# Where three steps ahead of a gated delta rule stand in the order of a fused two-block kernel

## What is computed

```python
q = jnp.repeat(l2_norm(q), rep, axis=2) * DN_HEAD_DIM ** -0.5
k = jnp.repeat(l2_norm(k), rep, axis=2)
...
decay = jnp.exp(jnp.where(incl, gc[..., :, None] - gc[..., None, :], -jnp.inf))
kk = jnp.einsum("bhncd,bhnjd->bhncj", k, k)
m = jnp.where(strict, beta[..., :, None] * kk * decay, 0.0) + jnp.eye(C, dtype=f32)
...
sol = lax.linalg.triangular_solve(m, rhs, left_side=True, lower=True, unit_diagonal=True)
```

```python
q = rms_norm(xq.reshape(B, S, XA_HEADS, XA_DIM), qn_g)
s = jnp.einsum("bthd,bmhd->bhtm", q, k).astype(jnp.float32) * XA_DIM ** -0.5
```

## Time and profile before

| | us |
|---|---|
| median of 3 runs | 3015.46 (3014.51 to 3021.64) |
| the profiled execution | 3011.83 |
| its span | 3010.0 |
| TensorE busy | 2836.4 (94%) |
| VectorE busy | 1903.9 (63%) |
| ScalarE busy | 1411.2 (47%) |
| GpSimd busy | 386.0 (13%) |
| mean granted clock of TensorE, as a share of 2.4 GHz | 0.973 |

### The profile page before, as it was taken

The page is one execution under the profiler, slowest core; times in us unless marked ns, Lnnn a source line. Parts: engine busy times, 40 slices in busy tenths (PEclk is TensorE's granted clock), DMA queues, the critical chain, the costliest instruction groups (busy, mean ns, idle before and its releaser), DMA issues.

```text
span 3010.0 us, 46274 instructions
## 1 busy us (share of the span) xinstructions
PE 2836.4 (94%) x19298; PEld 2672.0 (89%) x19298; DVE 1903.9 (63%) x2814; ACT 1411.2 (47%) x2387; POOL 386.0 (13%) x360
## 2 busy tenths in 40 slices
PE   6999989889889999999989999998999999999997
PEld 6999989888888998999979999997888899987785
DVE  5546648533323544655456865776888888878786
ACT  5346543555654433444344204343555555555454
POOL 0000010211111000003100002221122211112320
PEclk9999989999999999999999999999999999999998
DMA  4443444422223554444434458998999988899894
GB/s 185 169 154 140 169 131 167 154 77 94 85 94 112 198 186 166 167 169 162 154 114 169 156 204 322 374 357 312 366 361 371 366 319 322 321 350 349 319 350 147
DMA packets 109680, 668.46 MB, mean 222 GB/s; under 512 B 25777, under 2 KB 26313, under 8 KB 31553
## 3 DMA queue, kind: packets, MB, share of 16 engines
q1 hardware_dynamic: 83808, 496.08, 45.2%
q0 software_dynamic: 24512, 164.97, 15.0%
q10 hardware_dynamic: 1152, 4.47, 0.4%
HBM read 651.54 MB, written 13.30 MB: 221 GB/s over the span
## 4 chain that ended last, share of the span: by engine, by line
PE 72%; DVE 12%; DMA 8%; ACT 7%; issue 2%; POOL 0%; SPq 0%; DVEq 0%; ACTq 0%
PE PS L1027 71%; DMA raw<-in_pv 4%; DVE WL L1641 4%; DVE m L1632 3%; DMA m<-in_pv,keep 3%; ACT m L2322 2%; ACT WH L2337 2%; ACT L2322 1%; DVE m L1841 1%; DVE m L2162 1%; DMA raw<-in_w_kv 1%; DVE m L1838 0%; PE PS L1030 0%; ACT m L2323 0%; DVE m L1660 0%
## 5 line engine op out<-in xcount | busy, mean ns | idle before, releaser
L1641 DVE TENSOR_TENSOR WL<-raw,WH 128x1024 fp32r<-128x1024 f32 x804 | 985.5, 1234 | 650.6 <-ACT WH L2337 649.6
L2337 ACT CAST WH<-raw 128x1024 fp32r<-128x1024 f32 x804 | 837.5, 1046 | 551.5 <-PE PS L1027 390.2
L1027 PE MATMUL PS<-m_4096r,WH 128*128 128x256 f32 x5184 | 997.3, 293 | 29.9 <-DVE m L1632 14.7
L1027 PEld LDWEIGHTS PS<-m_4096r,WH 128*128 128x128 f32 x5184 | 827.8, 196 | 53.2 <-DVE m L1632 16.1
L1027 PE MATMUL PS<-m_4096r,WL 128*128 128x256 f32 x2592 | 743.6, 287 | 0.0
L1027 PE MATMUL PS<-m_8192r,WH 128*128 128x256 f32 (+1 forms) x2560 | 559.7, 312 | 17.5 <-issue 11.1
L1027 PE MATMUL PS<-WH,m_896r 128*128 128x512 f32 x1536 | 523.1, 393 | 28.2 <-DVE m_896r L2255 27.9
L1027 PEld LDWEIGHTS PS<-m_4096r,WL 128*128 128x128 f32 x2592 | 507.6, 196 | 0.0
L1027 PEld LDWEIGHTS PS<-m_8192r,WH 128*128 128x128 f32 x2560 | 397.6, 193 | 20.3 <-issue 11.7
L1027 PE MATMUL PS<-m_8192r,WL 128*128 128x192 f32 (+1 forms) x1792 | 404.3, 272 | 0.0
L1027 PE MATMUL PS<-WL,m_896r 128*128 128x512 f32 x1024 | 400.8, 391 | 0.0
(11 more groups left out here) (234 smaller groups left out, 1857.7 us busy)
## 6 DMA issues: line engine op xcount, KB each, us to landing
raw<-in_pu SPq DMA_DIRECT2D x128, 1024.0 KB, 6.8
raw<-in_pv SPq DMA_DIRECT2D x128, 1024.0 KB, 8.0
raw<-in_w_qkv SPq DMA_DIRECT2D x48, 1024.0 KB, 4.8
raw<-in_w_o SPq DMA_DIRECT2D x48, 1024.0 KB, 4.8
raw<-in_w SPq DMA_DIRECT2D x40, 1024.0 KB, 4.8
raw<-in_w_z SPq DMA_DIRECT2D x32, 1024.0 KB, 4.8
raw<-in_w_kv SPq DMA_DIRECT2D x16, 1024.0 KB, 4.8
raw<-in_w_q SPq DMA_DIRECT2D x16, 1024.0 KB, 4.8
```

Source lines behind the costliest of these rows:

```text
L1027: return e.matmul(o, l, x, start=start, stop=stop)
L1641: tt(WL[:, k, :], raw[:, n % NRAW, h * 1024:h * 1024 + 1024], WH[:, k, :].bitcast(F), ALU.subtract).then_inc(S["lo"], 1)
L2337: e.copy(WH[:, k, :], raw[:, n % NRAW, h * 1024:h * 1024 + 1024]).then_inc(S["hi"], 1)
```

## The change

- The cross attention's scores, and all steps of `cross` after them, come one yield later.
- The squares are summed two at a time with one eighth after each pair, instead of six with three eighths. From `rn_root` to `iv_turn` two eighths pass instead of none, and three follow instead of six. In all 17 eighths pass in `qk_norm` instead of 18.
- ScalarE's part of `iv_decay` is a step of its own, `iv_exp`, that comes later in the order than VectorE's differences. The eighths of `invert` stay 35 up to `iv_scale`.

Since `qk_norm` takes one eighth less, every later step up to the last group's end stands one eighth earlier against the units. No instruction is added or removed, on any engine.

```diff
     def cross(self):
         yield from self.head_norm("q")
+        yield
         for h in range(4):
...
     def qk_norm(self, st):
         for i in range(24):
             self.do("rn_sum", i)
-            if i % 6 == 5:
+            if i % 2 == 1:
                 yield
         self.do("rn_root")
+        yield
+        yield
         self.do("iv_turn")
+        yield
         yield
         yield
         st["n"] = True
...
         for b in range(3):
             self.do("iv_decay", b)
-            yield 3
-        yield 20
+            yield 2
+            if b:
+                self.do("iv_exp", b - 1)
+            yield 2
+        self.do("iv_exp", 2)
+        yield 17
...
         for _ in self.qk_norm(st):
-            for _ in range(3):
-                next(fz)
+            next(fz)
...
-            def iv_decay(b):
+            def iv_exp(b):
                 x = iv_e[:, b, :, :]
                 a.wait_ge(*at("iv_gap", b + 1))
                 a.step(act(x, x, ACT.Relu))
                 a.own()
                 act(x, x, ACT.Exp, scale=-1.0).then_inc(S["iv_exp"], 1)
```

More of the change, by code:

```diff
@@ L2714, in scalar_program @@
                   "v_out": v_out, "z_out": z_out, "rn_root": rn_root, "iv_turn": iv_turn,
-                  "iv_decay": iv_decay, "dn_decay": dn_decay, "dn_uc": dn_uc, "dn_w": dn_w, "dn_u": dn_u_, "dn_y": dn_y, "dn_yss": dn_yss,
+                  "iv_exp": iv_exp, "dn_decay": dn_decay, "dn_uc": dn_uc, "dn_w": dn_w, "dn_u": dn_u_, "dn_y": dn_y, "dn_yss": dn_yss,
                   "y_split": y_split, "x1_out": x1_out, "qi_out": qi_out, "index": index, "kq_out": kq_out,
```

## The result

| | before | after |
|---|---|---|
| median of 4 runs each, one chip, us | 3016.92 (3014.51 to 3021.64) | 2997.68 (2994.46 to 2999.27) |
| profiled execution: time, span, mean clock | 3011.83, 3010.0, 0.973 | 2994.46, 2992.7, 0.979 |

The account below looks back on a forecast made before the run. TensorE, busy 94% of the span, was taken as the bound, so its idle and low-clock time counts. Gains of 5.8 + 3.7 + 10.5 + 7 = 27 us from 3011.83 gave 2984.8, median forecast 2988.5, range 2977 to 3006.

Parts of the forecast that it names:

- B: Squares of `qk_norm` in pairs: the clock stays near 1.00 through them, gain 3.7 us; -13 if it falls.
- C: Exponentials in `invert` later: waits of 1.14 and 9.06 us go, gain 10.5 us, bounds 3 and 14.
- D: Groups one eighth earlier against the units: their waits change, gain 7 us, bounds -9 and 15.
- its own sign of being wrong: Prediction is wrong if squares' clock is near 0.5, unit 55's wait near 9 us, or groups together take longer.
- PE's waits on the reciprocals and on ScalarE: Sign to look for: TensorE's waits on L1889 and L2322 down from 35 us to 27 or less.
- Term A: Scores one yield later: the 2.99 us wait and 2.8 of low clock go, gain 5.8 us, lower bound 3.0.
- The new wait: Before unit 55, TensorE waits 3.7 us for ScalarE's Silu out of PSUM, with 2.5 of lower clock behind it.
- the wait at group 0: TensorE's 3.60 us wait at group 0 for the way over DRAM falls by 0.8.
- the rival that gave it: Groups don't gain: the eviction between block and waiting step takes all back, -9, so 3004 us; chance 0.12.
- the other six: Groups other than 1, 2, 5, 6, 9, 10: only TensorE's arrival moves, -0.7 us each, -4 together.
- slower, by the groups' evictions: Blocks don't start early, eviction and cast push the groups' waits, low clock follows: -30, so 3025 us; chance 0.05.
- The later stages: Stages after the change start when TensorE gets there, so a gain before 1000 us arrives at the end whole.

Follow-up runs that it names:

- squares_alone: Kernel before with only the squares summed in pairs, an eighth after each, and six eighths behind `iv_turn`, 18 in all; ratio to before 0.9966 (0.9945 to 0.9988).
- scores_alone: Kernel before with only the cross attention's scores one yield later; ratio to before 0.9997 (0.998 to 1.0014).
- squares_sixes: Changed kernel with the squares back in sixes and 18 eighths, so the groups stand where they did before; ratio to before 0.996 (0.9941 to 0.998).
- exps_alone: Kernel before with only the exponentials split off as their own step and put a block later; ratio to before 0.997 (0.9952 to 0.9988).

## Why the prediction was right, and where it was wrong

The side and the range were right: 2997.68 lies between 2977 and 3006. The forecast of 2988.5 was 9 us low; by the means of three profiles of after and two of before the sum of 27 is 12: 3.8 up to the first square, 13.6 to group 0, -7.1 in the groups, 1.8 behind them. (The eighth that moved from one stretch to the other is 0.7 of both the 13.6 and the -7.1.)

Part of this was luck. The 13.6 look like B and C together, 14.2, only because B was 3 to 4 us too small and C 4 too large. D had the wrong sign, by 14 us, which the range could hold because it reached down to rivals. And the prediction named its own sign of being wrong, that the groups together take longer; they did in all three profiles, by 7 us on the mean. PE's waits on the reciprocals and on ScalarE, to fall from 35 us to 27 or less, rose to 39.8 (21.2 and 18.6).

**Term A, 5.8.** Too large by 2.5 to 4.5. "Behind the scores nothing waits in the stage" was the step that failed: the turns and values came nearer to their VectorE work, and 2.50 of the 2.99 us came back as waits of 0.41, 1.40 and 0.69. The other 2.8 us, the low clock behind the wait, are real, but came in three of the four profiles with that wait. With low clock between 210 and 222 us in both, the first square comes at 371.1 with the wait and 368.0 without it, 3.1 apart; with none, squares_alone and scores_alone are 1.25 apart. Over all profiles the difference is 3.1 (366.6 for the ten with late scores, 369.8 for the four without). The gain did not add up with the rest where it stood alone: in scores_alone the collision described under squares_alone took 2.9 back.

**Term B, 3.7.** Too small: 7.8 from the first square to the tap of unit 50 (30.32 before, 22.56 after; 7.0 by the means), 8.4 to group 0 by squares_sixes. The mechanism was right: in the nine profiles with pairs the clock is 1.00 for 24 us from the first square, and in the five with sixes it falls. The count was wrong: I put 18 eighths into the 27.04 us, but its 170 records are 96 squares and 74 others, about 12 eighths of 6. At full clock that is 4 x 2.60 + 12 x 0.72 = 19.0, and 27.0 less 19.0 is 8. The row had the number in it. Of the Trainium skill's rule ("TensorE: Matmul & The Clock Gate", the section on the HAM clock gate), that the clock follows how busy TensorE is: the runs side with the row. PE is busy for 22.72 of 23.18 us in squares_alone's pairs at 1.00 and for 23.07 of 23.07 us in the sixes at 0.70. What differs is the length of the runs of one-column records.

**Term C, 10.5.** Right up to the first `iv_scale`, too large behind it. The new wait is 2.76 (forecast 3.7) with 0.60 of clock behind it, at unit 55 and behind the Silu, as worked out; `iv_scale` follows unit 50's tap by 35.4 us (forecast 36.5, before 46.2), 10.7 gained for 9.7. But from there to group 0 it takes 118.4 us for 114.4, so that from unit 50's tap to group 0 the gain is 6.9, and 6.6 by the means.

The exponentials alone bring 7 of the 10.7: exps_alone and squares_sixes have `iv_scale` 39.2 and 39.4 us behind unit 50's tap. The other 4 go with the eighth that `qk_norm` lost, since `iv_scale` then stands ahead of a low part whose cast comes late. VectorE in squares_sixes, then after:

```profile
430.26 3.50 DVE L1646 TENSOR_TENSOR WL<-raw,WH 128x1024 fp32r<-128x1024 f32 x3 [1.41 <-ACT WH L2342]
436.52 1.23 DVE L1646 TENSOR_TENSOR WL<-raw,WH 128x1024 fp32r<-128x1024 f32 x1 [2.77 <-ACT WH L2342]
437.66 1.21 DVE L1824 TENSOR_TENSOR m<-m,m 96x1024 f32<-96x1024 f32 x1
```

```profile
422.61 3.50 DVE L1648 TENSOR_TENSOR WL<-raw,WH 128x1024 fp32r<-128x1024 f32 x3 [1.40 <-ACT WH L2344]
426.03 1.22 DVE L1826 TENSOR_TENSOR m<-m,m 96x1024 f32<-96x1024 f32 x1
```

B and C seem not to add up alone: squares_alone gives 4.1 and exps_alone 5.9 against the mean of before, both together 13.6 with one eighth. The difference is the collision in squares_alone: with its 2.9 us added back, the two give 12.9, which is 13.6 less the eighth (an estimate).

One step failed: the wait at group 0, forecast to fall by 0.8, rose from 3.60 to 5.61. The pieces are in the timeline of POOL: from the issue of `s_it` to DRAM to the first product it takes 544.39 - 526.41 = 18.0 us, before 562.24 - 547.76 = 14.5. The two stores land 8.1 us after issue for 6.6, in the DMA list:

```profile
s_it<-m POOLq DMA_DIRECT2D x2, 384.0 KB, 8.1
```

This goes with the eighth, not with the exponentials. In the six profiles with 18 eighths in `qk_norm`, exps_alone among them, a load of weights is issued 4.8 us ahead of the stores and the next 0.9 behind, and the second store lands 7.2 to 8.3 us after issue. In the eight with 17 eighths the loads are issued 3.5 ahead (at 522.9 in after) and 1.6 behind, and it takes 9.8 to 10.8. That the loads slow the stores was not tested.

**Term D, 7.** The wrong sign: -7, near the bound of -9 and the rival that gave it. Three of the waits did shrink by the mechanism named, at group 2 (5.97 to 4.85), group 6 (4.86 to 3.54) and group 10 (5.22 to 4.18), though by about half of the 2.4 and 2.2; groups 1 and 5 gained 0.2 and 0.3, and the wait at group 9 grew (2.69 to 3.86). And the price of "the other six" was wrong. Only their arrival was to move, by 0.7; groups 4 and 8 got 0.7 and 1.4 more (2.55 to 3.29, 1.50 to 2.94), and small waits appeared where there were none. In the first pair of profiles the groups took 8.1 us more: PE's idle time grew by 2.1 us in all, and 0.7 is the eighth that moved in. What the sum had no line for was the clock: 5.3 us, the busy time less one eighth. Before, the 4 us behind 7 of the waits in the groups hold low clock, in both profiles; in after those behind 9, and 10 in its other two, the waits of 3.29 and 2.94 among them each time. The rival *slower, by the groups' evictions* carried such a term; the forecast itself, which moved twelve waits, did not.

**The later stages** "get the gain whole": on the mean, yes. But the rest took 2024 to 2041 us in 14 profiles of one and the same code, so one pair of profiles says nothing there to within 8 us.

## What to carry to other kernels

Check the count in a window's row before you put a formula on it: 170 records would have said 12 eighths. When waits of about 2 to 3 us move, add the low clock that can come with them to the sum; here waits that grew by about 1 us in a few places brought 5 us of it. And before tuning against totals, profile the unchanged kernel again and compare landmark to landmark: here the stretches inside the changed part repeat to 1 or 2 us, while single executions of before spread from 2993.27 to 3022.15. When a part that is tested alone brings less than in the whole, compare the durations of its instructions too: here one instruction of 1.6 us had become one of 4.5.

## What the hardware showed that I had not expected

- The same order of work with the same wait (2.99 us before the scores) was followed by low clock in three of the four profiles that have it and by none in the fourth. Those three also had low clock some 10 us ahead of the wait (0.69 in 210 to 220 us of before), the fourth did not (1.00).
- The length of a wait alone doesn't tell whether the clock falls: behind 2.55 it stayed at 1.00, in all nine profiles with the groups in their old place or one eighth back, and behind 2.94 it was 0.57 (0.64 and 0.66 in the other two profiles of after), but behind 2.99 in squares_alone it stayed at 1.00 and behind 2.22 in the changed kernel it was 0.65:

```profile
635.69:639.69 4.00, 4.00 (x21) 3.71 (x22) 2.34 (x4) 1.56 (x3) 0.00 (x0) 0.65 0.01 2
```

- A shift of the groups by one eighth (0.72 us of work, 28 to 29) shortens them from 422.3 to 424.0 us in three profiles to 419.4 and 416.8 in two; one of five eighths (28 to 33), which leaves five fewer in them, shortens them by nothing (422.8).
- A VectorE subtraction of 96x1024 that takes 1.22 us by itself took 4.51 and 4.55 us in the two profiles in which it began within 0.1 us of six GpSimd copies of 128x512 (3.39 us together).
